# Two late expert units added from SBUF by a 0/1 product, and the steps moved for it, in a hybrid recurrent, attention and mixture-of-experts block

## What is computed

```
h   = modulate(LN0(x), shift1, scale1)
mix = (g_rnn * (rg_lru(conv(h Wx)) * gelu(h Wy)) P_rnn + g_attn * diff_attention(h) P_attn) W_out
x   = LN(ALPHA * x + g1 * mix, ln1_g, ln1_b)
u   = modulate(LN0(x), shift2, scale2)
ffn = sum over the token's 8 experts of w * (silu(u Wg_e) * (u Wu_e)) Wd_e  +  shared expert(u)
x   = LN(ALPHA * x + g2 * ffn, ln2_g, ln2_b)
```

## Time and profile before

| | us |
|---|---|
| median of 3 runs | 1474.46 (1473.84 to 1480.21) |
| profiled execution, its own time | 1474.87 |
| its span, first to last instruction | 1473.1 |
| TensorE busy | 1330.3 (90%) |
| VectorE busy | 878.9 (60%) |
| ScalarE busy | 601.3 (41%) |
| GpSimd busy | 212.7 (14%) |
| DMA: read, written | 322.93 MB, 31.46 MB |

### The profile page before, as it was taken

One profiled execution on the slowest core, in us unless ns is written; L12 is line 12 of the kernel. 1 busy time (PEld: TensorE's weight loads), 2 busy tenths in 40 slices (PEclk: granted clock), 3 DMA queues, 4 the chain that ended last, 5 costly groups with the idle time before them and its releaser, 6 DMA issues.

```text
span 1473.1 us, 22049 instructions
## 1 busy us (share of the span) xinstructions
PE 1330.3 (90%) x6117; PEld 726.1 (49%) x6117; DVE 878.9 (60%) x1836; ACT 601.3 (41%) x845; POOL 212.7 (14%) x379
## 2 busy tenths in 40 slices
PE   1899999999998899998899999998999999999592
PEld 0677778866665677454333333333333333333231
DVE  6545776677777353567666666464566666565067
ACT  0445352345565221131254545444445454455300
POOL 1000000001100000000222222222122222221013
PEclk9999999999999899999799999999899999999887
DMA  8512446610110532334795889999998999993392
GB/s 307 197 58 86 143 161 222 216 58 30 58 58 1 193 126 91 128 143 151 267 345 202 346 294 372 403 392 376 396 366 318 346 365 340 402 392 137 102 386 97
DMA packets 131008, 334.05 MB, mean 227 GB/s; under 512 B 16153, under 2 KB 55186, under 8 KB 129938
## 3 DMA queue, kind: packets, MB, share of 16 engines
q1 hardware_dynamic: 111762, 283.11, 52.8%
q0 software_dynamic: 19200, 50.36, 9.4%
HBM read 322.93 MB, written 31.46 MB: 241 GB/s over the span
## 4 chain that ended last, share of the span: by engine, by line
PE 33%; DMA 11%; DVE 3%; issue 2%; SPq 1%; ACT 1%; POOL 0%; ACTq 0%; POOLq 0%; DVEq 0%
PE bank L1030 19%; DMA gu<-in_we_up 10%; PE bank L1050 9%; PE bank L1018 3%; PE bank L1009 1%; PE bank L1038 1%; SPq L526 1%; DVE y_sum L1908 1%; DMA y_all<-y_rows 1%; PE bank L1083 1%; DMA down<-in_we_down 1%; ACT down_use L1294 1%; DVE y_sum L1912 0%; SPq L434 0%; DVE stats L1915 0%
## 5 line engine op out<-in xcount | busy, mean ns | idle before, releaser
L1030 PE MATMUL bank<-gu_use,x_t 128*64 128x512 f32 x1664 | 380.9, 612 | 0.0
L1854 DVE COPY gu_use<-gu 128x1024 f32 x416 | 270.3, 709 | 76.9 <-DMA gu<-in_we_up 48.4
L1030 PEld LDWEIGHTS bank<-gu_use,x_t 128*64 128x64 f32 x1664 | 117.7, 140 | 218.6 <-issue 217.8
L1050 PE MATMUL bank<-down_use,act_t 128*64 128x512 f32 x832 | 191.6, 603 | 4.8 <-ACT down_use L1294 4.8
L1294 ACT ACTIVATE down_use<-down 128x2048 f32 x104 | 193.2, 1912 | 0.0
L763 PE MATMUL bank<-h_hi,w_lo 128*128 128x512 f32 x448 | 185.6, 414 | 4.0 <-DVE w_lo L1423 3.9
L765 PE MATMUL bank<-h_hi,w_hi 128*128 128x512 f32 x448 | 176.7, 394 | 0.0
L764 PE MATMUL bank<-h_lo,w_hi 128*128 128x512 f32 x448 | 176.5, 394 | 0.0
L1423 DVE TENSOR_TENSOR w_lo<-stream,w_hi 128x1024 fp32r<-128x1024 f32 x72 | 87.8, 1221 | 115.6 <-ACT w_hi L1103 115.5
L664 POOL DMA_INDIRECT y_rows<-y_item,y_index x52 | 53.3, 1026 | 467.0 <-ACT y_item L1320 457.2
L1818 DVE TENSOR_TENSOR pick<-slot_id,places 128x512 fp32r<-128x512 f32 x53 | 36.7, 692 | 134.4 <-POOL columns L676 134.1
(11 more groups left out here) (280 smaller groups left out, 1600.4 us busy)
## 6 DMA issues: line engine op xcount, KB each, us to landing
gu<-in_we_gate SPq DMA_DIRECT2D x128, 512.0 KB
gu<-in_we_up SPq DMA_DIRECT2D x128, 512.0 KB
down<-in_we_down SPq DMA_DIRECT2D x64, 1024.0 KB
stream<-in_w_in SPq DMA_DIRECT2D x28, 1024.0 KB, 5.2
ada_w<-in_w_ada POOLq DMA_DIRECT2D x8, 2048.0 KB, 9.6
y_all<-y_rows SPq DMA_DIRECT2D x8, 2048.0 KB, 14.2
ada_first<-in_w_ada SPq DMA_DIRECT2D x8, 1024.0 KB, 16.2
stream<-in_p_rnn SPq DMA_DIRECT2D x4, 1024.0 KB, 5.0
```

The lines of the kernel that those rows point to most:

```text
L1030: last = nc.tensor.matmul(bank[item.par][rows, :], x_t[:, k, rows], gu_use[h][:, :, k, :], start=(k == 0), stop=(k == KD - 1))
L1050: last = nc.tensor.matmul(bank[5 + half][rows, :], act_t[:, f, rows], down_use[h][:, f, cols], start=(f == 0), stop=(f == FE - 1))
L1854: last = V.tensor_copy(gu_use[h][:, b, ks, :], gu[:, bass.ds(slot, 1), b, ks, :].rearrange("p o k n -> p (o k) n"))
```

## The change

1. The results of the last two units are not scattered. After the loop, VectorE compares the lane numbers with the token numbers of these units' rows (`spot`, a 0/1 matrix of 128 places x 512 tokens per unit), and TensorE adds `spot` times `y_item` in the bank of each half tile. SP starts reading y_rows when the scatters of all other units have landed; the fourth buffer, which lies over `gu_use`, also waits for the last gate and up product.
2. The rows of y_rows that nobody writes must be zero. GpSimd clears `zeros` (which lies in `merged[:, 6:8]`) after the ninth sum of w_ada, and SP stores it eight times, behind the loads of the gr and pr blocks. VectorE waits for these stores before merge 6.
3. `result_out` moves from ScalarE to VectorE, behind `take_gu` part 1, and multiplies by g2. g2 also goes into `shared_down` once; the product by g2 per half tile (L1912) falls away.
4. TensorE adds 3 results instead of 4, VectorE 5. The first of them is fused with ALPHA * x, and the additions of half tile n+1 stand ahead of the bank's sum of n.
5. The final norm is two fused operations per half tile on VectorE, for all tiles; ScalarE's and GpSimd's passes fall away. ScalarE copies the first half of the last down weights, VectorE the second.
6. `lane`, a copy of the slot numbers, is made in the routing.

```diff
-BY_PE = 4
+BY_PE = 3
...
+                if kind in ("gr", "pr"):
+
+                    part = 2 * b + (kind == "pr")
+                    sp.wait_ge(zeros_ready, 1)
+                    sp.dma_start(y_rows[part * T:(part + 1) * T, :].rearrange("(j p) d -> p j d", p=P),
+                                 bcast(zeros[:, :], 1, NT)).then_inc(rows_zeroed, 16)
...
             for par in range(2):
                 sp.wait_ge(route_ready, 1)
-                sp.wait_ge(y_scattered[par], pairs * 16)
+                sp.wait_ge(y_scattered[par], (pairs - 1) * 16)
             sp.wait_ge(route_ready, 1)
             for n in range(2 * NT):
+                if n == 3:
+
+                    sp.wait_ge(gu_half, pairs * 4)
...
+            pool.wait_ge(acc_ready, 9)
+            nc.gpsimd.memset(zeros[:, :], 0.0).then_inc(zeros_ready, 1)
...
-                if not first:
+                if not first and not (end and item.par):
                     scatter(item.ahead(-1))
...
+            def sum_last(n):
+                if n == 0:
+                    pe.wait_ge(spot_ready, 2)
+                    wait(pe, y_out, last_item.n + 1)
+                for s in range(2):
+                    last = nc.tensor.matmul(bank[n % 4][:, :], spot[s][:, n // 2 * P:(n // 2 + 1) * P],
+                                            y_item[s][:, n % 2 * 512:(n % 2 + 1) * 512], start=False, stop=(s == 1))
                 last.then_inc(first_summed, 1)
...
+                if m == KD - 2:
+                    dve.wait_ge(rows_zeroed, 16 * 2 * NT)
...
+            def result_out(item):
+                wait(dve, y_done, item.n + 1)
+                wait(dve, y_scattered[item.par], item.pair * 16)
+                for half in range(2):
+                    cols = slice(half * 512, (half + 1) * 512)
+                    last = V.tensor_tensor(y_item[item.par][:, cols], bank[5 + half][:, :], g2_row[:, cols], ALU.mult)
+                last.then_inc(y_out, 1)
...
+            last_item = over_items(dve, step, plan)
+            wait(dve, y_done, last_item.n)
...
+            V.tensor_copy(down_use[1][:, :, :], down[:, bass.ds(slot, 1), :, :].rearrange("p o k n -> p (o k) n")
+                          ).then_inc(down_taken, 1)
+            dve.wait_ge(shared_down_in, 16)
+            for f in range(FE):
+                last = V.tensor_tensor(shared_down[:, f, :], shared_down[:, f, :], g2_row[:, :], ALU.mult)
+            last.then_inc(shared_scaled, 1)
...
+                for t in range(NT):
+                    last = V.tensor_scalar(spot[s][:, t * P:(t + 1) * P], lane[:, :], float(t * P), last_token[:, s:s + 1],
+                                           ALU.add, ALU.is_equal)
+                last.then_inc(spot_ready, 1)
+            result_out(last_item)
+
+            def rest_in(n):
+
+                dve.wait_ge(y_in[n % 4], 16 * (n // 4 + 1))
+                rest, part = y_all[n % 4], x1[:, n // 2, n % 2 * 512:(n % 2 + 1) * 512]
+                link(V.scalar_tensor_tensor(out=part, in0=part, scalar=ALPHA, in1=rest[:, BY_PE, :], op0=ALU.mult,
+                                            op1=ALU.add))
+                for k in range(BY_PE + 1, TOPK):
+                    link(V.tensor_tensor(part, part, rest[:, k, :], ALU.add))
...
+            rest_in(0)
+            for n in range(2 * NT):
+                if n + 1 < 2 * NT:
+                    rest_in(n + 1)
+                sum_in(n)
+                if n % 2:
+                    norm_out(n // 2)
```

More of the change, by code:

```diff
@@ L264, in hybrid_block @@
         columns = [at(f"columns{s}", 1.25 + 0.125 * s, [P, NT, 2, COLUMNS], F32R) for s in range(2)]
[L266 to L271, removed]
+        ln2g_row = at("ln2g_row", 22, [P, D])
+        ln2b_row = at("ln2b_row", 26, [P, D])
+        shared_down = at("shared_down", 30, [P, FE, D])
+        y_all = [at(f"y_all{s}", 38 + 16 * s, [P, TOPK, D // 2]) for s in range(4)]
+        zeros = at("zeros", 170, [P, D])
+        lane = at("lane", 201, [P, P])
+        last_token = at("last_token", 201.5, [P, 2])
+        spot = [at(f"spot{s}", 190 + 2 * s, [P, T]) for s in range(2)]
         params_in, x_in_s, rows_in, bd_in = sem("params_in"), sem("x_in_s"), sem("rows_in"), sem("bd_in")
@@ L698, in step @@
                     gather(item.ahead(2))
-                if not first:
+                if not first and not (end and item.par):
                     scatter(item.ahead(-1))
-            last_item = over_items(pool, step, plan)
-            scatter(last_item)
-            pool.wait_ge(ln2_in, 32)
+            over_items(pool, step, plan)
             for t in range(NT):
                 last_rstd(2 * NT + t)
[L708 to L713, removed]
         @block.tensor
@@ new lines, in sum_in, with norm_out @@
+            def sum_in(n):
+                part = x1[:, n // 2, n % 2 * 512:(n % 2 + 1) * 512]
+                dve.wait_ge(first_summed, n + 1)
+                V.tensor_tensor(part, part, bank[n % 4][:, :], ALU.add).then_inc(z_ready, 1)
+                dve.wait_ge(z_ready, n + 1)
+                link(V.bn_stats(stats[:, n // 2, n % 2, :], part))
+            def norm_out(t):
+                aggregate(t)
+                V.tensor_scalar(rstd[:, t:t + 1], moments[:, t, 1:2], LN_EPS, None, ALU.add).then_inc(var_ready, 1)
+                dve.wait_ge(ln2_in, 32)
@@ L1916, in _ @@
-                norm_terms(2 * NT + t)
-            dve.wait_ge(ln2_in, 32)
-            for half in range(2):
-                cols = slice(half * 512, (half + 1) * 512)
-                dve.wait_ge(x_ready, 3 * NT + half)
-                link(V.tensor_tensor(x1[:, NT - 1, cols], x1[:, NT - 1, cols], ln2g_row[:, cols], ALU.mult))
-                V.tensor_tensor(x1[:, NT - 1, cols], x1[:, NT - 1, cols], ln2b_row[:, cols], ALU.add).then_inc(last_ready, 1)
+                    last = V.scalar_tensor_tensor(out=x1[:, t, cols], in0=x1[:, t, cols], scalar=moments[:, t, 0:1],
+                                                  in1=ln2g_row[:, cols], op0=ALU.subtract, op1=ALU.mult)
@@ new lines, in norm_out @@
+                link(last)
+                dve.wait_ge(rstd_ready, 2 * NT + t + 2)
+                for half in range(2):
+                    cols = slice(half * 512, (half + 1) * 512)
+                    V.scalar_tensor_tensor(out=x1[:, t, cols], in0=x1[:, t, cols], scalar=rstd[:, t:t + 1],
+                                           in1=ln2b_row[:, cols], op0=ALU.mult, op1=ALU.add).then_inc(out_ready, 1)
+            rest_in(0)
+            for n in range(2 * NT):
+                if n + 1 < 2 * NT:
[3 more added lines that the diff above has]
+                    norm_out(n // 2)
```

73 lines of the change are left out of this document (29 added, 44 removed).

## The result

The changed kernel takes **1466.61 us** (median of 6 runs, 1459.98 to 1469.44), the kernel before 1474.15 us beside it (6 runs, 1467.35 to 1482.88). The ratio is 0.9937, 95% interval 0.9914 to 0.996. The forecast was 1455, its range 1449 to 1466. It is faster by 0.6%, where 1.3% was forecast, and lies 0.6 us above the range.

A forecast was written before the change was run, and what follows sets the result against it. It took TensorE to bound the expert loop, and waits for the last scatter and load, then VectorE, the tail. Tail -24.2, loop +3, attention +1 and lane copy +0.2 sum to -20.0: from 1474.87 to 1455 us, range 1449 to 1466.

The forecast's parts named there:

- The tail, -24.2: After the expert loop: y_all loads start earlier, small operations are hidden, VectorE runs unblocked; 24.2 us saved.
- The loop, +3: Expert units: the result's two operations move to VectorE, making some units late waiting for scatter landings; 3 us lost.
- The lead: In the loop: VectorE's copies end 3.5 us before TensorE needs them mid-product, absorbing three late units in a row.
- circle: In the loop: scatter landing, VectorE's copies, result, next scatter; 5.65 us plus the landing, against TensorE's period of 12.34.
- 16 times 0.9: In the loop: upper bound of the loss, 16 waits of VectorE for a landing at 0.9 us each, 15 us.
- landings would stay near the short ones: In the loop: by the page's rule of queue turns, the circle never reaches the period; 3 us less. Not followed.
- The attention, +1: Attention: eight added stores of zeros delay the first p_rnn load; 1 us lost, from 0 to 4.
- D: Attention: zeros not covered, the late p_rnn load costs 6 us more or the merge's wait binds; 1461 us, chance 0.05.
- A: Loop: the circle binds because landings grow by half a us; 1462 to 1466 us, chance 0.17.
- B: Loop: slower than before, the same circle with landings 1.5 us longer throughout; 1497 us, chance 0.06.
- C: Tail: TensorE binds, its clock at half through the first two half tiles; 1465 us, chance 0.06.
- E: Tail: the y_all loads still wait for something late; 1472 us, chance 0.01.

The follow-up runs named there:

- e1: c0 with the down product's result copied by ScalarE again, unscaled, and the product by g2 back in the tail: 1461.4 us, ratio 0.9913 to the kernel before.
- c0: Control: the changed kernel with each loaded number of the plan held at 0 or more before use: 1466.8 us, ratio 0.9955 to the kernel before.
- e8_index_behind_weights: c0 with y_index and its wait for the landing moved behind the slots' weights, ahead of the second half's copies: 1460.6 us, ratio 0.9892 to the kernel before.
- e2: c0 with y_index and its wait for the landing moved to the step's end, behind the result (one 128x1 copy): 1451.7 us, ratio 0.9832 to the kernel before.
- e3_before_vector: The kernel before, loaded numbers bounded, with only the result's two copies moved from ScalarE to the end of VectorE's step, unscaled: 1489.4 us, ratio 1.0126.
- e7: e2 with each of the eight stores of zeros issued twice, the second to a DRAM tensor nobody reads: 1453.1 us, one run.
- e6_again: e6_result_early repeated with more rounds: 1449.0 us, ratio 0.9818 to the kernel before.
- e10_last_two_stored: e2 with the last two units' results scattered again, y_all loads waiting for all scatters, their 0/1 products gone: 1465.8 us, ratio 0.9926 to the kernel before.
- e5_load_only: e1 plus, at the result's former place on VectorE, the same wait and two multiplications into a spare tile nobody reads: 1456.7 us, ratio 0.9897 to the kernel before.
- e6_result_early: c0 with VectorE taking the result out ahead of the second half's copies of the expert's weights: 1448.1 us, ratio 0.9809 to the kernel before.

## Why the prediction was wrong

**The tail, -24.2: right**, -24.4, and by its mechanism: loads issued with the second-last unit's end (1.03 us behind the start of its down product, forecast 2.8), landing after 9.9 (9.7), preparation hidden, VectorE at 0.69 to 0.72 throughout and done 55.8 us after the landing (56.9), TensorE not late. From VectorE's last operation to the span's end it is 7.3 us, though, not 4.9, so that the sum agrees to 0.2 is in part luck. (The last store lands 2 us after it in both kernels; what the program still does then takes 5.2 us, before 2.8, and I don't know why.) The experiments divide it. The last two results kept from the store are worth 13.4. g2 in the loop is worth 5.6 (e1's tail against c0's). The 5.4 that are left of 24.4 would be the fused norm and what else moved there, if the parts add up; I did not try that part alone.

**The loop, +3: wrong, and this is the step that failed.** The mechanism was named, and its length of 5.65 us and the landing is within 0.11 of what the trace of after shows. The term was mis-sized, 20.8 for 3, in three ways:
- *The lead.* "TensorE needs them in the middle of the product": the copies are not what TensorE first waits for. `pick_slots` needs `token_weight`, which stands between the wait and the copies. The timeline of before had it: `token_weight` done just ahead of the copies at 1198.72, and the picking product at 1200.67. The lead was 2 us, not 3.5. This row the forecast did not read:

```profile
1200.67 0.59 PE L1009 MATMUL bank<-columns,pick 128*128 128x8 f32 x4
```

  e8_index_behind_weights takes this link away: 9.0 us by the profiled loops, 6.2 by the medians.
- *What a lead does in a circle.* e8 has the lead as forecast, and still its loop is 11.6 us longer than e2's. The lateness stays on VectorE and reaches TensorE at `acted`. A lead delays when a circle longer than the period begins to cost; it does not pay for it unit after unit. I read the lead as holding "three late units in a row" and counted on short ones between; 36 of 50 landings were over the limit, and 30 of 50 were so in the kernel before.
- *The count.* "16 times 0.9" took the waits that VectorE had before, when the scatter left 1.45 us behind the start of a gate and up product (1188.85 to 1190.30); in the unit shown it is 4.09 (891.19 to 895.28). The changed kernel has 28 such waits. The landings are 0.75 us longer in the mean as well.

From the rule of the Trainium skill's page "DMA: Bandwidth & Descriptors", section "Queues, rings and completion order", the prediction took that landings would stay near the short ones. The trace of after speaks against that conclusion more than that of before did (7.92 in the unit shown, mean 7.00); no run here shows in what order an engine takes its queues.

**The attention, +1**: 0.3 by the two profiles, but 1.8 at an equal clock. The ninth sum of the w_ada blocks starts 1.33 us earlier than before (296.80 in the earlier trace rows, 295.47), the first `merged` 1.04 earlier (330.99 and 329.95): 0.3 lost between them. In this stretch, however, the kernel before had a drop of the granted clock that the changed one hadn't. e3_before_vector, which has the old kernel's loads and no zeros, hadn't it either. From 304 to 312 us (busy times of PE, PEld, DVE, ACT and POOL, granted clock, DMA share, GB/s), before, then e3_before_vector:

```profile
304.00:312.00 8.00, 6.64 (x38) 5.24 (x37) 6.07 (x19) 3.63 (x7) 0.00 (x0) 0.79 0.00 0
```

```profile
304.00:312.00 8.00, 6.64 (x49) 4.98 (x48) 5.59 (x19) 3.64 (x7) 0.00 (x0) 1.00 0.00 0
```

From the ninth sum to the first `merged`, e3_before_vector takes 1.8 us less than the changed kernel (295.55 to 328.21, against 295.47 to 329.95). Where the clock drops there, the zeros cost next to nothing: c0_bounded, at 0.79 as well, takes 34.3 us, the kernel before 34.2. The first p_rnn block's w_hi came at 313.56 instead of 310.63, between the 310 and 316 forecast; the seventh merge, behind the wait for the zeros, starts at 455.32 instead of 456.27, so that wait cost nothing. e7 shows that there is little room: D was a nearer miss than the 0.05 says.

**Rivals.** A, the circle binds, is what happened, by the mechanism given there, landings longer by more than half a us; its price, 10 to 14, was still too small, and that 1462 to 1466 came within 0.6 us is luck: a loop 21 us longer is outside it. It deserved more than 0.17: the likeliest case rested on a lead that had not been followed through the list of VectorE. B would have needed 1.5 us more per landing; it was 0.75. C did not occur: the granted clock was 1.00 from 1380 to 1410 us, and a half tile's seven products take 6.1 us (1400.98 to 1407.09). E did not occur: the loads leave early.

**Ahead of the loop**, -5.4 us was not forecast and is not the change's. Eleven profiled kernels that have the changed kernel's code up to there reached the first scatter at 730.0 to 738.2 us; the kernel before and e3_before_vector, with the old code, at 735.4 and 729.8. The traces differ in where the granted clock drops (us, then busy times of PE, PEld, DVE, ACT and POOL, granted clock, DMA share, GB/s). Before:

```profile
215.00:230.00 15.00, 14.83 (x60) 12.05 (x60) 13.62 (x15) 3.09 (x4) 0.19 (x1) 0.89 0.83 280
...
575.00:640.00 65.00, 62.31 (x181) 32.72 (x180) 34.86 (x56) 10.86 (x9) 4.31 (x11) 0.97 0.34 118
```

Changed:

```profile
215.00:230.00 15.00, 14.82 (x68) 12.27 (x68) 14.72 (x16) 3.10 (x4) 0.46 (x1) 1.00 0.84 280
...
575.00:640.00 65.00, 62.31 (x182) 32.18 (x181) 34.41 (x57) 9.80 (x8) 4.73 (x11) 1.00 0.34 118
```

Slowest of the eleven are e6_again and e10_last_two_stored (738.2 and 738.1), with 0.77 and 0.78 in the first of these stretches. In the second, all fourteen traces fall in two groups: the five at 1.00 take 254.4 to 256.0 us from the eighth merge to the first scatter, the nine at 0.97 take 258.2 to 259.6. Why the clock drops in one execution and not in another stays open. With the first stage of before (735.4) the profiled execution would have missed its forecast by 16 us, near the 17.8 of the loop's error. The medians, 7.5 us apart, are thus not the change's own size to the microsecond either: loop and tail, by one profile each, give 3.6.

## What to carry to other kernels

When an operation moves to another engine, follow what it releases, around to where that comes back: if a wait on the same engine stands between, its period is the sum around the circle, and it has to be held against the unit's period with the landing's usual length, not its shortest. A lead is an allowance for single late units only, and it is measured to the first thing behind the wait that anybody needs, not to the thing one thinks of first. The cure was cheap in both forms: put the wait behind the releasing operation (one 128x1 copy), or put the releasing operation ahead of work that can wait; either was worth 14 to 19 us here, twice what the change had gained.

## What the runs showed that was not expected

- A scatter of the same 128 rows seems to land later where VectorE's result releases it: the mean of the first 50 is 6.5 to 7.1 us in all such kernels, 6.3 to 6.4 in the three where ScalarE's does. The groups nearly touch (6.49 in e2_index_late, 6.42 in e5_load_only), and by their medians they overlap (7.25 in e7_zeros_twice, 7.28 in e5_load_only), with one profile each. Its place in the unit is not enough to explain it: in e6_result_early it leaves 1.7 us behind the start of the gate and up product (1190.13 to 1191.83), nearly as early as before (1.45), and the mean is 6.82. The cause stays open.
- Two stores of zeros ahead of one load of 1 MB held that load's reader up for 9.5 us, one for 4.1. What the first stores cost goes with the granted clock beside them: 1.8 us between two traces with no drop from 304 to 312 us, 0.1 between two with a drop to 0.79.
